# The causal mask of nine pairs of heads: added by VectorE in the banks, not by TensorE's products with an identity

## The reference

```python
def masked_softmax(s, mask):
    s = jnp.where(mask, s.astype(jnp.float32), -jnp.inf)
    m = jnp.max(s, -1, keepdims=True)
    ...
    e = jnp.where(mask, jnp.exp(s - m), 0.0)
    return e / jnp.maximum(jnp.sum(e, -1, keepdims=True), 1e-30)

# fox_mixer, 6 heads, in blocks of 128 queries
        s = jnp.einsum("bthd,bshd->bhts", qb, k).astype(jnp.float32) * scale
        s = s + cb[:, :, :, None] - cum[:, :, None, :]
        causal = kpos[None, :] <= tpos[:, None]
        p = masked_softmax(s, causal)
        return jnp.einsum("bhts,bshd->bthd", p.astype(v.dtype), v)
```

## Time and profile before

| | |
|---|---|
| median of 3 runs | 1248.15 us (1241.87 to 1249.3) |
| profiled execution, its own time | 1250.79 us |
| its span | 1249.0 us |
| TensorE busy | 1058.1 us, 85% |
| VectorE busy | 430.4 us, 34% |
| ScalarE busy | 234.7 us, 19% |
| GpSimd busy | 54.3 us, 4% |
| DMA | 323.66 MB, mean 259 GB/s |

### The profile page before, as it was taken

The page is one execution under the profiler, slowest core; times in us unless marked ns, Lnnn a source line. Parts: engine busy times, 40 slices in busy tenths (PEclk is TensorE's granted clock), DMA queues, the critical chain, the costliest instruction groups (busy, mean ns, idle before and its releaser), DMA issues.

```text
span 1249.0 us, 17841 instructions
## 1 busy us (share of the span) xinstructions
PE 1058.1 (85%) x7574; PEld 576.7 (46%) x7574; DVE 430.4 (34%) x1022; ACT 234.7 (19%) x578; POOL 54.3 (4%) x69
## 2 busy tenths in 40 slices
PE   5899999999999999999998989898766666666655
PEld 2344764444576447985667874442211111121111
DVE  0137646323864536255146763411000000000001
ACT  0012134101213504434112341210000000000001
POOL 0101000000100000000212310000000000000000
PEclk9999999999999999899998999799888988888898
DMA  9963338443345964014221004999999999999996
GB/s 384 380 263 135 118 124 338 164 151 135 135 142 238 428 271 152 1 68 155 92 94 70 3 2 150 365 397 429 429 429 432 429 429 432 430 428 429 433 428 255
DMA packets 27870, 323.66 MB, mean 259 GB/s; under 512 B 3232, under 2 KB 3360, under 8 KB 5776
## 3 DMA queue, kind: packets, MB, share of 16 engines
q1 hardware_dynamic: 25760, 314.18, 61.3%
q0 software_dynamic: 2032, 8.35, 2.0%
HBM read 321.47 MB, written 1.05 MB: 258 GB/s over the span
## 4 chain that ended last, share of the span: by engine, by line
PE 58%; DMA 30%; DVE 7%; issue 3%; ACT 1%; SPq 0%; POOL 0%; DVEq 0%; ACTq 0%; POOLq 0%
PE banks L634 48%; DMA ring<-in_stream 27%; DMA zuv_to_Kt<-in_stream 3%; PE banks L645 3%; PE banks L2157 1%; PE banks L895 1%; PE banks L881 1%; PE banks L916 1%; PE banks L878 1%; PE banks L782 1%; DVE probs L1239 1%; PE banks L886 0%; DVE KC L1231 0%; DVE scr_qk L2457 0%; SPq L541 0%
## 5 line engine op out<-in xcount | busy, mean ns | idle before, releaser
L634 PE MATMUL banks<-ring,uT 128*128 128x512 f32 (+1 forms) x512 | 224.4, 593 | 7.2 <-DMA ring<-in_stream 5.4
L634 PEld LDWEIGHTS banks<-ring,uT 128*128 128x128 f32 x512 | 95.9, 191 | 120.3 <-issue 110.9
L634 PE MATMUL banks<-ring,scr_qk 128*32 128x512 f32 (+1 forms) x576 | 101.3, 678 | 33.5 <-DMA ring<-in_stream 33.1
L634 PE MATMUL banks<-scr_qk 64*64 64x64 f32 (+4 forms) x2280 | 102.4, 258 | 16.4 <-DMA scr_qk<-in_stream 11.7
L634 PEld LDWEIGHTS banks<-scr_qk 64*64 64x64 f32 (+3 forms) x2280 | 82.5, 138 | 36.3 <-issue 16.5
L2667 DVE SCALAR_TENSOR_TENSOR UWK<-UWK,banks 128x256 f32<-128x256 f32 x16 | 6.7, 421 | 268.1 <-ACT UWK L2928 268.1
L634 PE MATMUL banks<-ring,UWK 128*32 128x512 f32 (+1 forms) x272 | 70.5, 671 | 10.0 <-DMA ring<-in_stream 6.5
L2928 ACT ACTIVATE UWK<-banks 128x256 f32<-128x256 f32 x16 | 6.1, 384 | 369.6 <-PE banks L634 369.6
L634 PEld LDWEIGHTS banks<-ring,scr_qk 128*32 128x32 f32 (+1 forms) x576 | 27.3, 127 | 100.4 <-DMA ring<-in_stream 51.7
L634 PE MATMUL banks<-UWK,ring 128*128 128x256 f32 x320 | 72.2, 386 | 0.0
L2157 PE MATMUL banks<-UWK 128*128 128x512 f32 x128 | 59.1, 604 | 13.3 <-DVE UWK L2675 13.3
(11 more groups left out here) (370 smaller groups left out, 1231.5 us busy)
## 6 DMA issues: line engine op xcount, KB each, us to landing
ring<-in_stream SPq DMA_DIRECT2D x94, 2048.0 KB, 13.8
scr_qk<-in_stream SPq DMA_DIRECT2D x11, 2048.0 KB, 38.9
Vt_to_O<-in_stream SPq DMA_DIRECT2D x11, 2048.0 KB, 38.9
zuv_to_Kt<-in_stream SPq DMA_DIRECT2D x11, 2048.0 KB, 39.4
wide<-in_stream SPq DMA_DIRECT2D x10, 1024.0 KB, 36.7
scr_qk<-in_stream SPq DMA_DIRECT2D x10, 1024.0 KB, 39.2
const<-in_stream SPq DMA_DIRECT2D x10, 1024.0 KB, 37.8
misc<-in_stream SPq DMA_DIRECT2D x10, 1024.0 KB, 39.2
```

What stands on the lines that cost most here:

```text
L634: return pe.matmul(o, a, b, start=start, stop=stop)
```

## The change

TensorE no longer adds the mask to the plain pairs: the two products of an identity with the mask in bf16 are gone, and the scores of a plain pair are complete after L881, whose products now carry the signal that the bank is full. VectorE adds the mask instead, in fp32, with one instruction for both heads, which reads the two diagonal blocks of both banks and writes them back; it then waits for its own addition before it takes the maxima. The dsa pairs stay as they were. The bf16 copy of the mask, which GpSimd made at the start, is gone too.

```diff
@@ pool_start
-            pool.tensor_copy(identb[:, :], ident).then_inc(*tick("pool_step"))
-            pool.tensor_copy(causb[:, :], C("causal")).then_inc(*tick("pool_step", "zeroed"))
+            pool.tensor_copy(identb[:, :], ident).then_inc(*tick("pool_step", "zeroed"))
@@ pe_scores
+            plain = kind != "dsa"
             for s, (r, qb, kb, _) in enumerate(heads):
                 q, k = TB[r:r + rows, qb, :], TB[r:r + rows, kb, :]
-                pe.matmul(bank[b + s][:, 0:P], q[:, 0:P], k[:, 0:P], start=True, stop=False)
+                pe.matmul(bank[b + s][:, 0:P], q[:, 0:P], k[:, 0:P], start=True, stop=plain)
             for s, (r, qb, kb, _) in enumerate(heads):
                 q, k = TB[r:r + rows, qb, :], TB[r:r + rows, kb, :]
-                pe.matmul(bank[b + s][:, P:384], q[:, P:SEQ], k[:, :], start=False, stop=False)
-            for s in range(2):
-                if kind == "dsa":
-                    ins = pe.matmul(bank[b + s][:, 0:384], identb[:, :], sel[:, :], start=False, stop=True)
-                else:
-                    ins = pe.matmul(bank[b + s][:, 0:384].rearrange("p (a n) -> p a n", n=P)[:, 0:3:2, :], identb[:, :],
-                                    times(causb[:, :], 2), start=False, stop=True)
-                ins.then_inc(*fill(b + s, "scores", l, m, s))
+                ins = pe.matmul(bank[b + s][:, P:384], q[:, P:SEQ], k[:, :], start=plain, stop=plain)
+                if plain:
+                    ins.then_inc(*fill(b + s, "scores", l, m, s))
+            if not plain:
+                for s in range(2):
+                    pe.matmul(bank[b + s][:, 0:384], identb[:, :], sel[:, :], start=False, stop=True).then_inc(*fill(b + s, "scores", l, m, s))
@@ v_max
+            if pairs[m][0] != "dsa":
+                own = banks[b][:, :, 0:384].rearrange("p s (a n) -> p s a n", n=P)[:, :, 0:3:2, :]
+                mask = C("causal").rearrange("p (s a n) -> p s a n", s=1, a=1).broadcast_to([P, 2, 2, P])
+                dve.tensor_tensor(own, own, mask, ALU.add).then_inc(*tick("vector_step"))
+                dve.wait_ge(*last("vector_step"))
             dve.tensor_reduce(mx[:, i, :, 0], banks[b][:, :, 0:P], X_AXIS, ALU.max, negate=True).then_inc(*tick("vector_step"))
             dve.tensor_reduce(mx[:, i, :, 1], banks[b][:, :, P:384], X_AXIS, ALU.max, negate=True).then_inc(*tick("vector_step", "max", l, m))
```

More of the change, by code:

```diff
@@ L355, in build @@
         sel = sb("sel", 384, dt=BF16, stack=one)
-        causb = sb("causb", P, dt=BF16, stack=one)
         probs = sb("probs", 3, 2, 384, stack=one)
```

## The result

The change makes the kernel slower: 1260.22 us median (1253.97 to 1262.28, 4 runs) against 1245.57 us (4 runs) on the same chip, 1.0084 times, with an interval of 1.0046 to 1.0122. Two later measurements of the same kernel on other chips gave 1.0053 [1.0021, 1.0086] and 1.0058 [1.0028, 1.0087]. The three average 1.0065, some 8 us. The forecast was 1247.0, within 1241.0 to 1252.5. The profiled execution after took 1258.82 us, 8.0 more than the one before.

What follows compares the result with a forecast made beforehand. TensorE was taken to bound layer 0's attention, full DMA loads the end of layer 1's. Terms of -0.56 us (layer 0) and -0.65 (layer 1) made -1.2, so 1247.0 us against the median 1248.15, range 1241.0 to 1252.5.

Steps and rivals of the forecast that it cites:

- What bounds the kernel: In layer 0 attention TensorE bounds; in layer 1 full DMA queues do until 441.52 us; a shift there reaches the end.
- a granted clock that falls in places where it didn't: Sign of being wrong, to be seen in the profile after: granted clock falling in new places; no size given.
- What goes from TensorE: Attention's plain pairs: two mask products fewer per pair, 36 in all, 3.05 us in layer 0, 6 us in all.
- What comes to VectorE: Before each plain pair's first maximum: one add of 0.69 us plus a wait of 0.03, 0.72 us.
- Rival B: VectorE's add costs 1.38 us because it writes where it reads: +1.3 us in total, 1249.4; chance 0.12.
- Layer 0: Layer 0's attention, pairs 0 to 8: savings and new waits sum to -0.56 us.
- The wait for gT: Layer 0, pair 2: TensorE's wait for VectorE grows from 2.6 to 3.3 us; everything up to the release comes +0.50 later.
- Behind pair 5: Layer 0: TensorE's next value product waits for ScalarE's copy, +0.39 us; pair 6's own saving falls into the wait.
- Pair 8's wait for ScalarE's copy: Layer 0, last plain pair: TensorE's next value product waits for ScalarE's copy, which comes 0.39 us later.
- Layer 1: Layer 1's attention: pairs 0 and 1 gain 0.65 us before the load burst; the rest hides behind full DMA queues.
- rival C: More TensorE idling (pairs 2, 5, 8; before layer 1's w_out) lowers its clock: +3.0 us, 1251.2; chance 0.17.
- The spread: Whole kernel: three earlier runs lie 7.4 us apart, about 0.6%; faster 0.02, same 0.96, slower 0.02.

Runs made afterwards that it cites:

- run 5: The changed kernel again, word for word, measured against the kernel before: 1258.32 us against 1249.85, 1.0053 [1.0021, 1.0086].
- run 6: The changed kernel with 18 tiny products added in each layer, giving TensorE the kernel before's instruction count: 1250.8 us, 1.0004 [0.9977, 1.003].
- run 12: The changed kernel without VectorE's adds, so no mask in plain pairs, with 18 tiny products in each layer: 1247.81 us, 1.0000 [0.9973, 1.0028].

## Why the prediction was wrong

By its own steps:

**What bounds the kernel.** "After 441.5 the chain is on TensorE and VectorE again [...] so a shift at 441.5 reaches the end." This is the step that failed. The shift that reached 591 us was +0.5, and +8.0 reached the end. I treated untouched stages as a fixed length. They are not: with the same code they differed by up to 10.8 us from one profiled execution to another (column "591 to end", +7.9 to -2.9), along with the time at half clock (41.0 against 20.5 us), and part of that follows from the number of instructions ahead of them: with the count restored the loss of 1.0053 became 1.0004 (runs 5 and 6). One of the prediction's own signs of being wrong, a granted clock that falls in places where it didn't, is what came.

**What goes from TensorE.** 36 products were priced by their own time alone. Their 72 instructions also stood in the stream, and taking them out moved all later code by 4.6 KB (72 x 64 bytes) against loads of 16 KB; that had no term. The products were also worth less than the 3.5 us that the prediction's prices gave for run 12: without any mask and at the old count nothing is gained (1.0000 [0.9973, 1.0028], run 12). By the Trainium skill's formula ("TensorE: Matmul & The Clock Gate", section "Back-to-back issue gap") the sum would have been -0.8 in place of -1.2, and as far off.

**What comes to VectorE.** 0.69 + 0.03 us forecast, 0.70 + 0.03 measured. Rival B, 1.38 us, is refuted.

**Layer 0.** The wait for gT at 3.3 us came as worked out. Behind pair 5 TensorE waited where the forecast had put a wait, but for another engine and for longer: 1.0 us for uT, not for ScalarE's copy. VectorE's step that writes uT is queued behind the add and the maxima, and TensorE's next value products need the bank that it empties. I had named it as queued there and not followed it to its reader. These products came 0.11 us early (192.05 for 192.16) where the forecast's sum stands at 0.62. Pair 8's wait for ScalarE's copy came, and took all of the 0.8 us that TensorE was ahead by then. -0.56 forecast, 0.0 measured.

**Layer 1.** The growth of the waits for DMA, "from 1.2 to about 2.6 us", came out at 3.5, but the cover was thinner than I had it: behind the longer wait the clock fell to half for 3.4 us and w_out's products came 0.5 us late, not 0.65 early. This is rival C's mechanism, in the place where C had put it. Its price for the whole was +3.0 us; what C did not have is the 6.7 us that go with lower clock in stages without a single changed instruction.

**The spread.** The range held only the attention's cases. The three runs before had shown 7.4 us between them, six times my sum. The ten executions of run 5, one and the same kernel, go from 1247.99 us at a granted clock of 0.940 to 1262.15 at 0.920 and 1264.62 at 0.923, so this spread goes with the clock. What moves the clock could move the median by as much, and it belonged in the bounds.

## What to carry to other kernels

When a change adds or removes many instructions on an engine that runs dense groups of short ones, everything behind it moves against the loads of code; look for stalls on nothing ahead of dense groups, and measure the change once with its instruction count restored by empty ones (here 18 tiny products a layer turned +0.5% into +0.04%) before you believe either its gain or its loss. Take the work away altogether, at equal count, before you move it: that run (12) would have said at once that there were at most some 3 us to win. And a single profile compares stages of lower clock by chance: take the stage from the trace, but the size from the medians.

## What the runs showed of the hardware that was not expected

- TensorE can stall 1.0 to 2.4 us with no semaphore to wait for among dense 64x64 products (192 in 5.9 us). The stall stands behind 5825, 6082, 6338, 6849 or 7105 products and weight loads from the program's start, whole loads of 256 apart to within one, and 256 instructions more bring it back to the same products. It ends 1.2 to 1.5 us after a 16 KB packet of the instruction queue has landed (20 stalls in 18 traces).
- Which edge stalls is not decided by the code ahead alone: two kernels that are the same up to there stalled behind 5825 and 6849, and behind 6849 only.
- How long the clock stays at half over the same 96 products depended on when it fell: 17.1 us where it fell 2.3 to 2.5 us after their start (four profiles), 3.4 us and then 3.4 us again where it fell 3.0 to 3.9 us after it (eleven).
- VectorE reads a bank and writes it back in place at the price of a read: 0.70 us for 128x512 fp32, with 0.03 us more for a dependent maximum.
- The same 96 fp32 products of 64x64 took 10.22 us with the clock at half for 3.4 us of it, and 13.98 with it at half for 11.6 us of it.
